# Experts of the three fullest groups as three products of rounded parts, in a fused two-block transformer kernel

## The reference

```
# x: 256 tokens x 1024; 32 experts in 8 groups of 4, d_expert = 256
scores = sigmoid(x @ w_router)                 # a group is chosen for each token, then 2 of its 4 experts
hid    = silu(xb @ w1[e]) * (xb @ w3[e])       # xb: the tokens of expert e; w1, w3: 1024 x 256
ys     = hid @ w2[e]                           # w2: 256 x 1024
y[tok] += ys * gate
x      = layer_norm(ALPHA * x + y, ln2_g, ln2_b)
```

## Time and profile before

| what | value |
|---|---|
| median of 3 runs | 2347.69 us |
| lowest, highest | 2339.07, 2348.42 us |
| time of the profiled execution | 2344.33 us |
| its span, first to last instruction | 2341.3 us |
| what lies around the span | 3.0 us |
| mean granted TensorE clock | 0.971 |
| PE busy, DVE busy, ACT busy | 2189.8, 968.1, 609.6 us |
| experts of layer 0: round 0 to end of round 25 | 1360.1 to about 1682 us |
| experts of layer 1 | 2005.6 to about 2328 us |

### The profile page before, as it was taken

How to read it: one execution, slowest core, us unless ns; L and a number is a source line. 1 busy time by engine, 2 the same in 40 slices (tenths; PEclk the granted TensorE clock), 3 DMA queues, 4 the chain that set the end, 5 groups by cost and what they waited for, 6 DMA issues and landing times.

```text
span 2341.3 us, 26628 instructions
## 1 busy us (share of the span) xinstructions
PE 2189.8 (94%) x11048; PEld 1574.2 (67%) x11048; DVE 968.1 (41%) x1533; ACT 609.6 (26%) x985; POOL 60.2 (3%) x98
## 2 busy tenths in 40 slices
PE   5999999999997889999999899999899998899997
PEld 3667778756686669979998753334499987533343
DVE  3333332525443246566655631121466556311213
ACT  3111222312212134444544210010145432100100
POOL 0000000100000000000000200000000002000000
PEclk8999999999997999999999989999899999899998
DMA  9555331222221144535434168879354341678892
GB/s 371 234 222 219 146 135 59 103 90 77 104 108 37 44 155 180 185 119 179 143 109 162 49 269 330 337 320 392 140 183 145 109 162 49 269 319 338 325 387 103
DMA packets 53879, 433.47 MB, mean 185 GB/s; under 512 B 7169, under 2 KB 8449, under 8 KB 17537
## 3 DMA queue, kind: packets, MB, share of 16 engines
q1 hardware_dynamic: 49904, 423.35, 47.0%
q10 hardware_dynamic: 3856, 8.42, 1.0%
HBM read 430.71 MB, written 1.05 MB: 184 GB/s over the span
## 4 chain that ended last, share of the span: by engine, by line
PE 60%; issue 35%; DVE 2%; ACT 1%; DMA 1%; DVEq 1%; POOL 0%; POOLq 0%; SPq 0%; ACTq 0%
PE bank L2596 18%; PE bank L3259 10%; PE bank L2589 9%; PE bank L3261 5%; PE bank L3312 5%; PE bank L3314 3%; PE bank L2533 1%; PE bank L3327 1%; PE bank L3223 1%; PE bank L2740 1%; PE bank L2698 1%; DMA ring<-in_early 1%; PE bank L3278 1%; PE bank L3291 1%; PE bank L2710 1%
## 5 line engine op out<-in xcount | busy, mean ns | idle before, releaser
L2596 PE MATMUL bank<-X_HI,ring_lo 128*128 128x256 f32 x1472 | 267.6, 282 | 2.1 <-issue 2.1
L2596 PE MATMUL bank<-HT_HI,W_HI 128*128 128x512 f32 (+1 forms) x704 | 239.2, 340 | 8.5 <-DVE ring_lo L1662 4.3
L2596 PE MATMUL bank<-HT_HI,ring_lo 128*128 128x512 f32 (+1 forms) x704 | 240.0, 341 | 0.0
L2596 PE MATMUL bank<-HT_LO,W_HI 128*128 128x512 f32 (+1 forms) x704 | 238.0, 338 | 0.0
L2596 PEld LDWEIGHTS bank<-X_HI,ring_lo 128*128 128x128 f32 x1472 | 228.0, 188 | 3.5 <-issue 3.4
L2596 PE MATMUL bank<-HT_LO,ring_lo 128*128 128x256 f32 x736 | 207.2, 281 | 0.0
L1064 ACT ACTIVATE W_HI<-ring 128x2048 fp32r<-128x2048 f32 x66 | 126.4, 1915 | 295.0 <-PE bank L2596 228.7
L3259 PE MATMUL bank<-ring,TOKENS 128*128 128x512 f32 x416 | 192.4, 606 | 3.6 <-issue 3.6
L2482 DVE SCALAR_TENSOR_TENSOR tmp<-th,bank 128x256 f32<-128x256 f32 x50 | 21.1, 421 | 411.9 <-ACT th L1443 411.9
L1662 DVE TENSOR_TENSOR ring_lo<-ring,W_HI 128x2048 fp32r<-128x2048 f32 x66 | 151.0, 2288 | 53.0 <-ACT W_HI L1064 53.0
L2019 DVE TENSOR_TENSOR ring_lo<-ring,ring_lo 128x2048 fp32r<-128x2048 f32 (+2 forms) x64 | 143.2, 2247 | 45.1 <-ACT ring_lo L1258 44.0
(11 more groups left out here) (483 smaller groups left out, 3195.1 us busy)
## 6 DMA issues: line engine op xcount, KB each, us to landing
ring<-in_early SPq DMA_DIRECT2D x64, 2048.0 KB, 8.2
ring<-in_l_moe_in SPq DMA_DIRECT2D x38, 2048.0 KB, 12.6
ring<-in_l_dense SPq DMA_DIRECT2D x62, 1024.0 KB, 4.9
ring<-in_l_moe_out SPq DMA_DIRECT2D x12, 2048.0 KB, 11.9
slot<-in_l_moe_in SPq DMA_DIRECT2D x10, 2048.0 KB, 9.3
HT<-in_l_moe_in SPq DMA_DIRECT2D x8, 2048.0 KB, 10.7
slot_xg<-in_l_moe_in SPq DMA_DIRECT2D x8, 2048.0 KB, 11.1
ring<-in_l_moe_out SPq DMA_DIRECT2D x14, 1024.0 KB, 11.4
```

The costliest lines, as they stand in the source:

```text
L2596: last = mm(out, a, b, start=start and n == 0, stop=stop and n == 2)
```

## The change

Whole steps, except the two of rank 0's first expert (14 of 16 in each layer), get their products as three products of rounded parts, in `up` and in `down`.

- Tokens are rounded once a rank: ranks 0 in round 1, ranks 1 and 2 in round 14 (`TOKENS_AT`), ACT then DVE, 2048 columns for rank 0 and 1024 each for the others.
- Each of the 11 experts concerned has its weights rounded in 8 pieces: 4 of 1024 columns ("in") and 4 of 512 ("out"). ACT writes the high part to memory that is idle at the time, DVE writes the rest in place. The high parts have room for one expert, so a piece waits until the previous expert's use of that room is over.
- Where the pieces stand: in the round before the expert's first step, two of the "in" pieces before the tanh and gate of that round and two behind (all four behind, if the step before is not such a step); the four "out" pieces in the round of its first step, behind the "in" pieces of the next expert.
- In DVE's round the pieces behind the gate stand ahead of the scatter adds and of the `DOWN_PARTS` subtraction.
- The transposed hidden tile becomes two parts, by ACT and then DVE.
- The rows `ln2_g`, `ln2_b`, whose room is now used, are loaded in round 24 on ACT's queue, after its "out" pieces.

```diff
+SPLIT_RANKS = (0, 1, 2)
...
+        SPLIT_STEP = [h.size == P and h.rank in SPLIT_RANKS and (h.rank, h.step) != (0, 0) for h in HIDDEN]
...
+        for x, n in enumerate(EXPERT_STARTS):
+            early = 2 if SPLIT_STEP[n - 1] else 0
+            BEFORE_TANH[n - 1] += [(x, "in", q) for q in range(early)]
+            AFTER_TANH[n - 1] = [(x, "in", q) for q in range(early, 4)] + AFTER_TANH[n - 1]
+            AFTER_TANH[n] += [(x, "out", q) for q in range(4)]
...
 @block.scalar
+                def round_piece(piece):
+                    x, what, q = piece
+                    h = HIDDEN[EXPERT_STARTS[x]]
+                    unit_loaded(se, L, (h.ins if what == "in" else h.outs)[0])
+                    if x:
+                        last_use = EXPERT_ENDS[x - 1]
+                        if what == "out":
+                            unit_freed(se, L, HIDDEN[last_use].outs[0])
+                        elif q < 2:
+                            se.wait_ge(up_half_done, L * N_SPLIT_STEPS + sum(SPLIT_STEP[:last_use + 1]))
+                        else:
+                            filled(se, at(L, J_UP[last_use]))
+                    w, w_hi, _ = piece_parts(piece)
+                    act(w_hi, w, ACT.Copy).then_inc(expert_rounded, 1)
...
                 for n in range(N_HIDDEN + 1):
-                    if n:
-                        evac(HIDT[:, (n - 1) % 2, :], J_TURN[n - 1], PS[J_TURN[n - 1][0]][:, 0:T])
+                    if n and SPLIT_STEP[n - 1]:
+                        filled(se, at(L, J_TURN[n - 1]))
+                        act(HIDT_PARTS[:, 0, :], PS[J_TURN[n - 1][0]][:, 0:T], ACT.Copy).then_inc(hidt_rounded, 1)
+                    elif n:
+                        evac(HIDT, J_TURN[n - 1], PS[J_TURN[n - 1][0]][:, 0:T])
+                    if n < N_HIDDEN:
+                        for piece in BEFORE_TANH[n]:
+                            round_piece(piece)
...
+                    for r in TOKENS_AT.get(n, ()):
+                        round_tokens(r)
+                    if n < N_HIDDEN:
+                        for piece in AFTER_TANH[n]:
+                            round_piece(piece)
+                    if n == EXPERT_ENDS[-1]:
+                        load_rows2()
...
 @block.vector
+                def subtract_piece(piece):
+                    ve.wait_ge(expert_rounded, L * N_PIECES + PIECE_NUMBER[piece] + 1)
+                    w, w_hi, w_lo = piece_parts(piece)
+                    tt(w_lo, w, w_hi, ALU.subtract).then_inc(expert_split, 1)
...
                 for n in range(N_HIDDEN + 1):
+                    if n and SPLIT_STEP[n - 1]:
+                        ve.wait_ge(hidt_rounded, L * N_SPLIT_STEPS + sum(SPLIT_STEP[:n]))
+                        tt(HIDT_PARTS[:, 1, :], PS[J_TURN[n - 1][0]][:, 0:T], HIDT_PARTS[:, 0, :],
+                           ALU.subtract).then_inc(*free(J_TURN[n - 1]))
                     if n < N_HIDDEN:
+                        for piece in BEFORE_TANH[n]:
+                            subtract_piece(piece)
...
+                    for r in TOKENS_AT.get(n, ()):
+                        subtract_tokens(r)
+                    if n < N_HIDDEN:
+                        for piece in AFTER_TANH[n]:
+                            subtract_piece(piece)
                     if n == N_HIDDEN and L < LAYERS - 1:
                         subtracts(L + 1, 0, 1)
                     for step in SCATTERS[n]:
                         add(*step)
...
 @block.tensor
+                def split_up(n, part):
...
+                    for q in (2 * part, 2 * part + 1):
+                        w_hi, w_lo = pieces_ready(n, "in", q)
+                        for a in range(2):
+                            k, cut = 2 * q + a, slice(a * BANK, a * BANK + BANK)
+                            last = three(ps[:, :], TOK_HI[:, k, own], TOKENS_LO[:, k, slots], w_hi[:, cut], w_lo[:, cut],
+                                         k == 0, k == KD - 1, tokens_first=True)
+                    last.then_inc(*(full(J_UP[n]) if part else (up_half_done, 1)))
+
+                def split_down(n):
...
+                    taken(J_TURN[n])
...
+                        for f in range(2):
+                            w_hi, w_lo = pieces_ready(n, "out", 2 * half + f)
+                            cut = slice(f * P, f * P + P)
+                            last = three(by_two(ps[:, :]), HIDT_PARTS[:, 0, cut], HIDT_PARTS[:, 1, cut], w_hi, w_lo,
+                                         h.first and f == 0, h.last and f == 1, tokens_first=True)
```

More of the change, by code:

```diff
@@ L261, in build_program @@
         sb("x_tokens", [P, 2, D])
-        slot_xg = sb("slot_xg", [P, 4096])
-        sb("ln2_rows", [P, 2, D])
+        with ExitStack() as raw:
+            slot_xg = raw.enter_context(nc.sbuf_tensor("slot_xg", [P, 4096], fp32))
+        slot_xg_lo = sb("slot_xg_lo", [P, 4096], fp32r)
+        IN_HI12 = sb("IN_HI12", [P, 2, D], fp32r)
         cols = sb("cols", [P, N_COLS])
@@ L274, in build_program @@
         rope1 = sb("rope1", [P, 2, 2, 32])
-        th = sb("th", [P, 2, BANK])
-        tmp = sb("tmp", [P, 2, BANK])
-        junk = sb("junk", [P, BANK])
+        with ExitStack() as raw:
+            th = raw.enter_context(nc.sbuf_tensor("th", [P, 2, BANK], fp32))
+            tmp = raw.enter_context(nc.sbuf_tensor("tmp", [P, 2, BANK], fp32))
+            junk = raw.enter_context(nc.sbuf_tensor("junk", [P, BANK], fp32))
+        th_parts = sb("th_parts", [P, 2, BANK], fp32r)
+        tmp_parts = sb("tmp_parts", [P, 2, BANK], fp32r)
+        junk_part = sb("junk_part", [P, BANK], fp32r)
         sc = sb("sc", [P, KD, 2])
@@ L335, in build_program @@
         X_PARTS = sb("X_PARTS", [P, 2, 2, D], fp32r)
-        sb("experts_arena", [P, 2816])
-        TOKENS = sb("TOKENS", [P, KD, N_SLOTS])
+        sb("hidg_arena", [P, 2 * T])
+        HIDT_PARTS = sb("HIDT_PARTS", [P, 2, T], fp32r)
+        IN_HI3 = sb("IN_HI3", [P, D], fp32r)
+        OUT_HI3 = sb("OUT_HI3", [P, BANK], fp32r)
+        sb("gates_arena", [P, 256])
+        with ExitStack() as raw:
+            TOKENS = raw.enter_context(nc.sbuf_tensor("TOKENS", [P, KD, N_SLOTS], fp32))
+        TOKENS_LO = sb("TOKENS_LO", [P, KD, N_SLOTS], fp32r)
         PLACE_T = sb("PLACE_T", [P, STATIONS, T], fp32r)
@@ L345, in build_program @@
             IOTA = early.enter_context(nc.sbuf_tensor("IOTA", [P, PLACE_COLS], fp32))
-        slot4 = sb("slot4", [P, 4096])
+        with ExitStack() as raw:
+            slot4 = raw.enter_context(nc.sbuf_tensor("slot4", [P, 4096], fp32))
+        slot4_lo = sb("slot4_lo", [P, 4096], fp32r)
+        TOK_HI = sb("TOK_HI", [P, KD, T], fp32r)
+        IN_HI0 = sb("IN_HI0", [P, D], fp32r)
         def region(start, *dims):
@@ L684, in build_program @@
                 FREED.append(("free", free_counts[u % RING2]))
+        SPLIT_STEP = [h.size == P and h.rank in SPLIT_RANKS and (h.rank, h.step) != (0, 0) for h in HIDDEN]
+        EXPERT_STARTS = [n for n in range(N_HIDDEN) if SPLIT_STEP[n] and HIDDEN[n].ins != HIDDEN[n - 1].ins]
+        EXPERT_ENDS = [n for n in range(N_HIDDEN) if SPLIT_STEP[n] and (n + 1 == N_HIDDEN or HIDDEN[n].ins != HIDDEN[n + 1].ins)]
+        TOKENS_AT = {}
+        for r in SPLIT_RANKS:
+            first = next(n for n in EXPERT_STARTS if HIDDEN[n].rank == r)
+            TOKENS_AT.setdefault(1 if r == 0 else next(n for n in EXPERT_STARTS if HIDDEN[n].rank == 1) - 2, []).append(r)
+        BEFORE_TANH, AFTER_TANH = [[] for _ in HIDDEN], [[] for _ in HIDDEN]
+        for x, n in enumerate(EXPERT_STARTS):
[3 more added lines that the diff above has]
+            AFTER_TANH[n] += [(x, "out", q) for q in range(4)]
+        PIECE_NUMBER = {}
+        for n in range(N_HIDDEN):
+            for piece in BEFORE_TANH[n] + AFTER_TANH[n]:
+                PIECE_NUMBER[piece] = len(PIECE_NUMBER)
+        N_PIECES, N_SPLIT_STEPS = len(PIECE_NUMBER), sum(SPLIT_STEP)
+        EXPERT_OF = {n: x for x, (a, b) in enumerate(zip(EXPERT_STARTS, EXPERT_ENDS)) for n in range(a, b + 1)}
         LAYER_USES = [n - m for n, m in zip(jobs.used, before_layers)]
@@ L900, in gate_part, with piece_parts, token_parts, unit_loaded @@
             return X[:, 2 + i // 2, i % 2 * BANK:i % 2 * BANK + BANK].rearrange("p (a n) -> p a n", a=2)
+        def piece_parts(piece):
+            x, what, q = piece
+            h = HIDDEN[EXPERT_STARTS[x]]
+            s = (h.ins if what == "in" else h.outs)[0] % RING2
+            if what == "in":
+                cut = slice(q * D, (q + 1) * D)
+                return RING[s][:, cut], IN_HI[q], RING_LO[s][:, cut]
+            cut = slice(q % 2 * D + q // 2 * BANK, q % 2 * D + q // 2 * BANK + BANK)
+            return by_two(RING[s][:, cut]), OUT_HI[q], by_two(RING_LO[s][:, cut])
+        def token_parts(r):
+            own = slice(0, T) if r == 0 else slice((r - 1) * P, r * P)
+            cut = slice(SLOTS_AT[r], SLOTS_AT[r] + (T if r == 0 else P))
+            return TOKENS[:, :, cut], TOK_HI[:, :, own], TOKENS_LO[:, :, cut]
```

(38 more changed lines are left out.)

38 lines of the change are left out of this document (31 added, 7 removed).

## The result

The changed kernel takes 2360.1 us (median of 6 runs, 2355.8 to 2364.5) against 2345.7 for the kernel before on the same chip: a ratio of 1.0063, with an interval of 1.0049 to 1.0077. It is 14 us slower. The forecast was 2347, no change that can be told.

The account below looks back on a forecast made before the run. PE, busy 94% of the span, was taken as the bound, the transfer queue nearly as full. From 2344.3 us: -54.9 for cheaper products, +46.1 waits, +11.4 clock gave +2.6, 2347 us; its own range 2335 to 2356, overall 2327 to 2362.

Parts of the forecast that it names:

- the gain: PE, whole steps: 0.163 us saved a product, 1.96 a step, 27.4 a layer, 54.9 for both layers at most.
- The plain product's 0.857: PE: one plain product of 512 columns takes 0.857 us, against 0.694 for three rounded ones.
- the waits: PE waits a layer in rounds 14, 15, 17, 20, 21, 22, 25; sum 22.6 and 23.5 us, 46.1 for both.
- the extra 0.9 that I gave to layer 0's end: Round 25, layer 0: 0.9 us more, the next layer's two subtractions standing behind the hidden tile's.
- the terms written down (0.83 + 4x0.61 + 0.4): Round 20: 3.8 us from the end of `down(18)` to the start of `down(19)`, 1.0 now; 2.6 wait.
- So the waits of rounds 17, 21 and 22 (5.5, 6.1, 3.9) cost 1.9 each on top: 6 x 1.9 = 11.4: PE after these waits: products at half clock lose 1.9 us each time, 11.4 for both layers.
- a bound: Upper bound on the clock's loss: rounds 20 and 25 also lose it, five of five waits, 19 us instead of 11.4.
- The slower one: Rival: the transfer queue is further behind, units land later in rounds 17 and 21; 2357, up to 2364 us; chance 0.18.
- "Only the order, transfers early": Rival: only program order makes waits, 17.3 and 18.2 us a layer; 12 to 19 faster, 2325 to 2332; chance 0.19.
- The dear product: Rival: three-part rounded products are no cheaper than plain ones, break-even 0.286 us a product; 2390 us; chance 0.02.
- the queue was 0.90 to 1.02 busy: Transfer queue before the change, at slower rounds: cited against the rival that transfers are early.
- full gain: Rival: all waits are hidden, so the whole 55 us is gained; 2289 us; chance 0.03.

Follow-up runs that it names:

- rank 0 alone: The changed kernel with only rank 0's 6 whole steps a layer in parts, ranks 1 and 2 plain fp32: 2320.0 us, ratio 0.9890 to the kernel before.
- adds first: The changed kernel with DVE's adds of each round's first two scatters moved ahead of token and weight pieces: 2322.6 us, ratio 0.9901 to the kernel before.
- rank 7's half: The changed kernel loading only the first half of each rank 7 weight, used for both halves: 2349.9 us, ratio 1.0012 to the kernel before.
- all pieces behind the tanh: Changed kernel, first two adds ahead of pieces, plain down in steps 19 and 24, ranks 1 and 2's input pieces behind tanh and gate: 2306.2 us, the fastest.
- the plain `down`s: The changed kernel with the first two adds ahead of pieces and plain fp32 down in steps 19 and 24: 2314.0 us, ratio 0.9866 to the kernel before.
- The fill: The changed kernel plus unused dummy rounded products on PE in the gaps of rounds 17, 20, 21, 22, 25: 2346.7 us, ratio 1.0005 to the kernel before.

## Why the prediction was wrong

**Right: the gain.** 0.231 a product, 11.1 us in rounds 1 to 14, and for rank 0 alone 23.0 us in both layers by the rounds (25 by the medians). The plain product's 0.857 is 0.860 by the rows that it names (3.44 us for four), which changes the sum by 1 us.

**Right: the waits.** Forecast 0.6, 1.6, 5.5, 2.6, 6.1, 3.9 and 2.3; measured in layer 0, net of the 0.56 that was there, 0.3, 1.4, 5.5, 2.9, 6.2, 3.9 and 2.5: 22.7 against 22.6. Layer 1 has 5.2 and 6.1 in rounds 17 and 21 and is alike otherwise; the extra 0.9 that I gave to layer 0's end wasn't there. In round 20 the terms written down (0.83 + 4x0.61 + 0.4) give 3.7 and not 3.8, with 1.0 taken off 2.7 and not 2.6; it measured 2.9. Their causes are shown too: the order by adds first, rank 7's share of round 21 by rank 7's half, the late unit's share of round 17 by all pieces behind the tanh, the ends by the plain `down`s.

**The step that failed: "So the waits of rounds 17, 21 and 22 (5.5, 6.1, 3.9) cost 1.9 each on top: 6 x 1.9 = 11.4".** The mechanism was right, the term was too small, for two reasons.
- The clock fell behind all five long waits, not three. Twelve products after each take 4.27, 4.3, 4.53, 4.50 and 4.45 instead of 2.77: 8.2 us a layer, where I took 5.7. Each fall cost less than the 1.9 I took. I had left out rounds 20 and 25 although my own row had a fall after 2.74 us of idle time, and their waits with the 0.56 are 3.4 and 3.1. I had kept them as a bound.
- The second scatters run at half clock too, 1.87 for four. In the fastest kernel, where they follow `down` without a gap at full clock, they take 0.91 (first line to second):

```profile
1585.15 1.07 PE L3500 MATMUL bank<-DOWN_PARTS,PLACE_T 128*128 128x512 f32 x4
1586.06 0.39 PE L2729 MATMUL bank<-IN_HI,TOK_HI 128*128 128x512 f32 x1
```

Behind a gap at full clock they take 1.17, as in round 15 of the changed kernel: the second pair starts 0.60 behind the first, as the second add does. So 0.7 of the 0.96 is the clock's, three times a layer 2.9 with both. No term had it.

Together 11.1 a layer instead of 5.7. By the rounds of the two profiles the change cost 13.4 us, where the sum had 2.6: 10.8 short. The products are 5.0 of it, these scatters 5.8, the scatters of rounds 14 and 15 another 0.8; the waits were 1.0 less than forecast. That adds up within 0.2. The fill gave 13 of the 22 back, where it couldn't cover the gaps whole. It is no rule, though, that every such wait costs this: one of 3.21 us in the kernel with rank 7's half cost nothing beyond itself.

**The rivals.** The slower one, with its time of 2357 to 2364, gave the right time for the wrong reason: its landings were to be 2.5 to 4 us later than I had them, and ACT waited 4.27 and 3.76 us, as I had worked out (to 0.2 us in round 21). "Only the order, transfers early" had the order right. The dear product is refuted by the spacing of 0.231.

**A step that I didn't take.** I read that the queue was 0.90 to 1.02 busy and didn't draw the end from it: by the estimate above full gain was not only unlikely but out of reach in rounds 17 to 21, where PE was to save four steps' 7.8 us and the queue had 4.2 to give. For the change as made it decided little; it decides what a better order can reach, and it ate about half of two repairs.

## What to carry to other kernels

When work goes to an engine that another one waits for, first place the small operation that frees a bank ahead of the new bulk, and keep loads that may be late behind the operations that others wait for: here the same arithmetic is 14 us slower in one order and (with two plain `down`s) 40 us faster in another. Price each wait of some 2 us or more between dense matmuls with its slow restart, all of them, small ones beside big ones too; here it was between nothing and some 2.5 us, so give it a range. When a repair brings less than its sum, look one or two rounds later for the same microseconds, and set the bytes of the stretch against the queue's rate before believing any gain on PE.

## What the runs showed of the hardware

- Rounded products of 512 columns: the clock stayed at 2.4 GHz behind all waits of 1.43 to 1.64 us that I looked at, and fell to 1.2 behind 1.92, 2.06, 2.32, 2.60 and nearly all longer ones, at once or within about a microsecond of the restart. But behind 3.21 (rank 7's half, layer 0) it stayed up. So the length doesn't decide alone; what does is not shown here.
- Twelve products behind a wait lost 1.5 to 1.8 us in the changed kernel, hardly more behind 6.2 us than behind 3.1. In other kernels they lost 0.5 behind 2.60 (three at 0.43, then 0.23), 0.45 behind 6.66, and 2.1 behind 3.42.
- The Trainium skill (TensorE: Matmul & The Clock Gate, "What's actually happening") says that activity releases the throttle, and that the number of slow products differs from run to run. The rows agree: the clock comes back while PE is busy, and the two layers of one profile differ (twelve products in 2.78 and in 4.33 us in round 21 of the kernel with rank 7's half). The next section of that page gives 426.7 ns for 512 columns at the lower clock, as here, and 215.7 at the higher, where these rows show 231.
- The queue held 427 to 434 GB/s over whole rounds when it was full (430 before, 434 changed, 429 with plain ends, 427 in the fastest).
- The attention of the first block keeps a half clock for some microseconds more or less from profile to profile, in unchanged code, enough to move the start of the experts by up to 7 us (1 us early to 6 us late against the kernel before).
